# A new order of the engines' items in the attention periods of a two-block kernel

## What is computed

```python
def first_block(x, ...):
    h = rms_norm(x, norm_mix[l])
    proj = h @ w_in[l]                      # q, kc, vc, ks, vs, kw, vw, gates, hq, hf, hi, hg
    o_nsa = nsa_mixer(q, kc, vc, ks, vs, kw, vw, gates)     # compressed, selected and window branch
    o_hgrn = hgrn2_mixer(hq, hf, hi, hg, lower_bounds[l], hgrn_o_norm[l])
    x = x + concatenate([o_nsa, o_hgrn]) @ w_out[l]
    h = rms_norm(x, norm_ffn[l])
    gate, up = split(h @ w_gate_up[l])
    return x + (silu(gate) * up) @ w_down[l]

def second_block(x, ...):
    for l in range(2):
        proj = rmsnorm(x, attn_norm[l]) @ w_in[l]           # sb_q, sb_k, sb_v, df_q, df_k, df_v
        sb_out = stick_breaking_attention(sb_q, sb_k, sb_v)
        df_out = rmsnorm(differential_attention(rope(df_q), rope(df_k), df_v, lam), subln_norm[l])
        x = x + concatenate([sb_out, df_out]) @ w_o[l]
        x = x + square(relu(rmsnorm(x, mlp_norm[l]) @ w_ff1[l])) @ w_ff2[l]
    return rmsnorm(x, final_norm)
```

## Time and profile before

| | us |
|---|---|
| median of three runs | 1956.21 |
| lowest and highest | 1955.7 to 1957.72 |
| the profiled execution | 1955.69 |
| its span in the profile | 1953.9 |
| PE busy in the span | 1923.8 |
| a middle period of the first block | 65.4 |
| LAST1's stretch | 63.0 |
| LAST2's stretch, one layer | 42.8 |

### The profile page before, as it was taken

One profiled execution on the slowest core, in us unless ns is written; L12 is line 12 of the kernel. 1 busy time (PEld: TensorE's weight loads), 2 busy tenths in 40 slices (PEclk: granted clock), 3 DMA queues, 4 the chain that ended last, 5 costly groups with the idle time before them and its releaser, 6 DMA issues. The chain is left out here.

```text
span 1953.9 us, 25592 instructions
## 1 busy us (share of the span) xinstructions
PE 1923.8 (98%) x9150; PEld 1510.5 (77%) x9150; DVE 916.7 (47%) x1420; ACT 834.5 (43%) x1269; POOL 881.6 (45%) x1188
## 2 busy tenths in 40 slices
PE   9999999999999999999999999999999999999998
PEld 7866766788888887777688888887777688888887
DVE  5487877432241346777541313133777643222132
ACT  4466555543242345555532223134555542222233
POOL 4322221456456465343355455454443355454543
PEclk9999999999999999999999999999999999999999
DMA  8211111233234233222134233333222223243322
GB/s 234 65 44 44 34 44 33 87 106 110 84 89 119 76 96 99 75 66 75 48 107 116 78 108 97 87 97 95 78 66 76 65 85 110 86 119 86 109 86 76
DMA packets 318100, 168.77 MB, mean 86 GB/s; under 512 B 15028, under 2 KB 313367, under 8 KB 317847
## 3 DMA queue, kind: packets, MB, share of 16 engines
q1 hardware_dynamic: 314432, 162.38, 28.9%
q10 hardware_dynamic: 3542, 4.76, 1.0%
HBM read 160.29 MB, written 2.10 MB: 83 GB/s over the span
## 5 line engine op out<-in xcount | busy, mean ns | idle before, releaser
L737 POOL TENSOR_TENSOR wlo<-raw,whi 128x256 fp32r<-128x256 f32 x1164 | 865.2, 775 | 1042.2 <-ACT whi L778 1042.2
L1621 PE MATMUL accs<-Xh,whi 128*128 128x512 f32 x1448 | 581.3, 401 | 0.1
L1623 PE MATMUL accs<-Xh,wlo 128*128 128x512 f32 x1448 | 565.1, 390 | 0.0
L1622 PE MATMUL accs<-Xl,whi 128*128 128x512 f32 x1448 | 563.9, 389 | 0.0
L778 ACT ACTIVATE whi<-raw 128x1024 fp32r<-128x1024 f32 x291 | 307.7, 1061 | 267.6 <-PE accs L1623 218.5
L1621 PEld LDWEIGHTS accs<-Xh,whi 128*128 128x128 f32 x1448 | 272.1, 188 | 58.6 <-issue 3.7
L1623 PEld LDWEIGHTS accs<-Xh,wlo 128*128 128x128 f32 x1448 | 271.8, 188 | 58.4
L1622 PEld LDWEIGHTS accs<-Xl,whi 128*128 128x128 f32 x1448 | 272.4, 188 | 56.1 <-issue 3.6
L1621 PE MATMUL accs<-Uh,whi 128*128 128x512 f32 x744 | 289.7, 389 | 0.8 <-DVE xT L1210 0.8
L1622 PE MATMUL accs<-Ul,whi 128*128 128x512 f32 x744 | 289.4, 389 | 0.0
L1623 PE MATMUL accs<-Uh,wlo 128*128 128x512 f32 x744 | 289.4, 389 | 0.0
(11 more groups left out here) (303 smaller groups left out, 1913.8 us busy)
## 6 DMA issues: line engine op xcount, KB each, us to landing
raw<-in_w_ff_dram SPq DMA_DIRECT2D x128, 512.0 KB
raw<-in_w_in_dram SPq DMA_DIRECT2D x71, 512.0 KB
raw<-in_w_gate_up_dram SPq DMA_DIRECT2D x44, 512.0 KB
raw<-in_w_down_dram SPq DMA_DIRECT2D x16, 512.0 KB
raw<-in_w_o_dram SPq DMA_DIRECT2D x16, 512.0 KB
px<-W ACTq DMA_DIRECT2D x64, 64.0 KB, 2.0
raw<-in_w_down_dram SPq DMA_DIRECT2D x8, 384.0 KB
W<-in_x_dram SPq DMA_DIRECT2D x4, 512.0 KB, 6.1
```

The costliest lines, as they stand in the source:

```text
L737: pool.tensor_tensor(lo[:, ks], raw[:, unit_no % RAW, ks], hi[:, ks].bitcast(F32), ALU.subtract).then_inc(sems["wlo"], 1)
L1621: mmul(y, whi[:, slot, k], xh[:, k], start=(i == 0), stop=False)
L1622: mmul(y, whi[:, slot, k], xl[:, k], start=False, stop=False)
L1623: last = mmul(y, wlo[:, slot, k], xh[:, k], start=False, stop=(i == len(ks) - 1))
```

## The change

The lists ORDER, LAST1 and LAST2 are written anew. The items are the same and each stands there as often as before; ORDER2 and all the code that the engines run are unchanged. One line is added ahead of that code, so each line number of it is one higher after the change (L1340 is L1341).

```diff
 ORDER = [
-    ("n1", 0, 0, 0), ("n4", -1, 1, 3), ("ca2", 0), ("mixo", -1), ("hn2", -1), ("ha1", 0), ("mmB", 0, "hi"), ("n1", 0, 0, 1),
-    ("mmA", 0, "hg"), ("vt", 0), ("hd", 0), ("vt2", 0, "hv"), ("cb", 0), ("ha2", 0), ("n1", 0, 0, 2), ("mmB", 0, "hg"), ("hD", 0, 0),
...
-    ("n4", 0, 1, 1), ("n4", 0, 1, 2), ("silu2", 1, "hq"), ("n3", 0, 1, 3), ("hn1", 0), ("mmA", 1, "hi"),
+    ("n1", 0, 0, 0), ("mmB", 0, "hi"), ("ca2", 0), ("hn2", -1), ("n4", -1, 1, 3), ("ha1", 0), ("n1", 0, 0, 1), ("vt", 0), ("hd", 0),
+    ("mmA", 0, "hg"), ("vt2", 0, "hv"), ("cb", 0), ("ha2", 0), ("mixo", -1), ("n1", 0, 0, 2), ("hD", 0, 0), ("n2", 0, 0, 0),
...
+    ("silu", 1, "hq"), ("ca1", 1), ("n4", 0, 1, 1), ("n4", 0, 1, 2), ("silu2", 1, "hq"), ("hn1", 0), ("n3", 0, 1, 3),
+    ("mmA", 1, "hi"),
 ]
 LAST1 = [
...
 LAST2 = [
-    ("rope", 3, 0), ("s3", 3, 1), ("s1", 3, 3), ("dfr", 3, 1), ("mmA", 3, "dv"), ("s3", 3, 2), ("dv", 2), ("mmB", 3, "dv"),
-    ("early", 0, 0), ("s2", 3, 3), ("rope", 3, 1), ("d1", 3, 0), ("early", 0, 1), ("vt", 3, "dfv"), ("d1", 3, 1), ("d2", 3, 0),
...
+    ("s3", 3, 1), ("rope", 3, 0), ("s3", 3, 2), ("dfr", 3, 1), ("s1", 3, 3), ("rope", 3, 1), ("mmA", 3, "dv"), ("mmB", 3, "dv"),
+    ("d1", 3, 0), ("early", 0, 0), ("early", 0, 1), ("s2", 3, 3), ("early", 0, 2), ("d1", 3, 1), ("dv", 2), ("vt", 3, "dfv"),
...
 ]
```

More of the change, by code:

```diff
@@ L273 @@
 LAST1 = [
-    ("n1", 3, 0, 1), ("vt", 3), ("mmA", 3, "hg"), ("hd", 3), ("hD", 3, 0), ("ha2", 3), ("n1", 3, 0, 2), ("mmB", 3, "hg"),
-    ("hD", 3, 1), ("n2", 3, 0, 0), ("n1", 3, 0, 3), ("vt2", 3, "hv"), ("silu", 3, "hg"), ("early", 0, 0), ("n2", 3, 0, 1),
-    ("early", 0, 1), ("hu1", 3), ("early", 0, 2), ("cb", 3), ("hu2", 3), ("early", 1, 0), ("early", 1, 1), ("early", 1, 2),
[7 rows of a table removed]
[10 rows of a table added]
 ]
 LAST2 = [
[5 rows of a table removed]
-    ("early", 2, 2), ("d3", 3, 3), ("early", 2, 3), ("dv", 3), ("early", 1, 5), ("on1", 3), ("early", 0, 5), ("early", 2, 4),
-    ("early", 1, 6), ("early", 2, 5), ("early", 0, 6), ("early", 2, 6), ("on2", 3),
[5 rows of a table added]
+    ("early", 2, 2), ("d3", 3, 3), ("early", 2, 3), ("dv", 3), ("early", 1, 5), ("on1", 3), ("early", 2, 4), ("early", 2, 5),
+    ("early", 0, 5), ("on2", 3), ("early", 2, 6), ("early", 1, 6), ("early", 0, 6),
 ]
```

## The result

| | us |
|---|---|
| before, median of 18 runs | 1956.74 (1955.37 to 1958.57) |
| after, median of 18 runs | 1960.24 (1959.34 to 1961.58) |
| ratio | 1.0018, 95% interval 1.0012 to 1.0025 |
| span of the profiled execution, before and after | 1953.9 and 1958.5 |

The forecast was 1955.0, "no change", between 1950.8 and 1958.8. The time is 1.4 us above the range. It is slower, though by less than the 3.9 us that the text called no change.

A forecast was written before the change was run, and what follows sets the result against it. TensorE is 98% busy, so only its short waits, mostly for VectorE, can be won. Heads -1.44, ends -0.5, LAST1 -0.6 and LAST2 +1.3 sum to -1.24 us: forecast 1955.0, no change, range 1950.8 to 1958.8.

The forecast's parts named there:

- Heads: Heads of periods 1 and 2: vT ready 0.72 us earlier, so PE's wait before the v transposes goes; -1.44 in all.
- Ends: Ends of periods 0 to 2: hn1's 0.17 us wait for the square L966 goes; -0.5 in all.
- LAST1: Last period of the first block: waits of 2.8 us go, new ones come; -0.6 us (-1.5 to +0.8).
- hF 4: LAST1: only one early step now stands between scores n1 13 and hF4, so PE stops; +1.3 us.
- n3 0 0: LAST1: scalings n2 01 run beside POOL's split, +1.27 us, mostly covered by early steps ahead of the transposes; +0.3 (0 to 0.7).
- LAST2: Last period of each second-block layer: -2.35 us of waits gone, new ones added; +0.65 per layer (-0.35 to +2.15).
- d1 0: LAST2: these scores, directly behind mmB dv, wait for transfers, Abs, L1501 and rotary; +1.0 us per layer (+0.7 to +1.5).
- s3 33: LAST2: shares d1 1's buffer and waits for its exps, delayed by scans and s2 33's exp; +0.8 us (0.5 to 1.4).
- rival B: LAST2: DVE's queue becomes the bound, some 3.5 us per layer; slower, 1960.7 us; chance 0.14.
- A: LAST2: transfers leave before Abs, rotary 31 ready, s3 33 not held; -1.15 us per layer, faster, 1951.3; chance 0.24.
- C: Heads: scores n1 03 wait for the exps of n1 02, so 0.72 us comes back; no change, 1956.4; chance 0.12.
- D: LAST1: port lock holds each of four scalings for a whole POOL part, 3.3 us; no change, 1958.0; chance 0.04.

The follow-up runs named there:

- the single lists: Three kernels, each the kernel before with one new list: ORDER 1955.04 us, LAST1 1956.63, LAST2 1959.62, beside 1956.15.

## Why the prediction was wrong

- **What bounds the kernel** was right: small waits of PE, mostly for DVE, and a result of a few us.
- **Heads**: right. 0.72 was forecast for each of two periods, 0.78 measured, and alone 0.69 and 0.80.
- **Ends**: the sign right, the size short: 0.17 forecast, 0.37 measured, within the bounds.
- **The step that failed first is the one that isn't there.** The sum has terms for the head and the end of a period and none for its middle. There silu moved behind hD 1, and by the prediction's own row a collision of POOL's split with four scalings costs 1.27 us of DVE; 0.53 of it came back, since hF's two steps were freed from the same split. I asked where a collision would be new in LAST1 only, and in ORDER looked at the lists of PE and DVE, not at ACT's split, which sets when POOL starts. 0.73 in each of three periods, 2.2 us, turned a gain of ORDER of 2.7 into 0.5. Of the 4.7 us between the sum and the stages the periods make up 1.4 (these 2.2, less what heads and ends gave beyond the forecast), LAST1 1.5 and LAST2 1.8.
- **LAST1**: the waits that go were about right (2.8 forecast, 3.2 measured, from the starts of each item and the next). Two new terms were too small: hF 4 cost 1.75 in place of 1.3, and n3 0 0 1.1 in place of 0.3. I had the collision there, but counted the scalings alone: the copy of cb (L1316) stands behind them on DVE, and n3 0 0 needs its buffer. The small breaks made up 1.2 in place of 0.65. With +0.88 the stretch came out just above its bound of +0.8.
- **LAST2**: the waits that go were right (2.33, forecast 2.35), the pair of transposes too (0.95 and 0.13 behind it). d1 0 cost 1.24 and 0.97 (forecast 1.0, where the transfers' landing, not in the sum, added 0.56), s3 33 0.99 and 1.28 (0.8), the later items about 0.6 (0.25). The terms for d1 0 and s3 33 were taken in the lower part of their ranges, and of all open terms only d1 0 in the second layer didn't come out above: +1.5 to +1.6 per layer, inside the stated -0.35 to +2.15, but far from the +0.65 in the sum. For s3 33 the step that failed is the same as in the periods: the sum has the scans at 2.48 us, and beside POOL's split they took 2.84 and 3.09. Without these 0.36 and 0.61 the term would have been 0.63 and 0.67. The prediction had that collision in rival B, not in its sum. No run took the split away from the scans; it is read from the times of the four layers above.
- **Rivals**: A is out; the transfers do stand ahead of Abs and cost 2.70 us of ACT. C is out. D is out: the scalings took 3.20, not over 4. B named the right queue, and the scans did stretch beside POOL, to between 2.84 and 3.38 and not to 4.1; its price was 3.5 per layer, the runs show 1.5 to 2.1.
- **The range** is narrower than the prediction's own bounds. Heads 0 to -1.46, ends 0 to -1.74, LAST1 -1.5 to +0.8 and LAST2 -0.7 to +4.3 add up to -5.4 and +5.1, which is 1950.8 to 1961.3 on the scale of the forecast, and 1960.24 lies inside. The text put them at about -3.5 and +4 and ended the range at 1958.8, without saying why the upper end of LAST2 could be left out. Nor did it leave room for a stretch that hadn't been read.

## What to carry to other kernels

In a list that several engines walk, an item that moves also moves what is hung on its neighbours: here a weight conversion on ACT, which nobody waits for, set when GpSimd starts, and that stretched VectorE work that PE waits for by two thirds. At both of its places in a period the split ran beside some step of VectorE; the place decided which step paid, and how much. So after each move ask of every engine what now runs beside what, in every stretch where the order differs, and let the sum have a term for each. And cover for one wait is taken from the next when both hang on one chain: shorten the chain, or spread the fill along it.

## What was not expected of the hardware

In the same place of LAST2 the granted clock of TensorE fell, not in each run. After the stop of 3.40 us it was 0.50, which is the lower level of 1.2 GHz, and 1.00 again from 947 us on. In the kernel with the changed ORDER and silu back, where LAST2 is the old one, PE had stopped for 0.54 and 0.91 us within 3 us, and then:

```profile
930.00:932.00 2.00, 1.09 (x9) 0.64 (x7) 1.12 (x2) 1.18 (x5) 2.00 (x4) 1.00 0.02 5
932.00:934.00 2.00, 2.00 (x9) 1.25 (x10) 0.69 (x1) 0.00 (x0) 1.52 (x3) 0.57 0.86 257
934.00:936.00 2.00, 2.00 (x5) 1.07 (x4) 0.96 (x4) 1.13 (x4) 0.00 (x0) 0.58 0.52 155
936.00:938.00 2.00, 2.00 (x15) 1.78 (x14) 0.40 (x1) 1.61 (x3) 0.00 (x0) 1.00 0.36 108
```

That layer's stretch took 43.80 us in place of 42.2. Where mixo alone was moved, the first layer had stops of 0.51 and 0.91 us, the clock fell as well, and the stretch took 43.78. With the same two stops the kernel with the changed ORDER alone kept the full clock, and so did the kernel before with longer ones, 1.10 and 0.91. So two short waits there cost more than their length in some executions; what decides it stays open. The spread between executions goes with the clock: of 33 executions of the kernel before, measured beside the single lists, 12 had a mean granted clock of 0.998 or less and took 1956.49 to 1961.32 us, the other 21 took 1954.94 to 1956.48. Where in those executions the clock fell is not recorded.

And the collision is paid on both sides: POOL's four parts took 2.79 us in their old place and 3.31 beside the scalings, while the scalings went from 1.93 to 3.20.
